# Weight ring of a float32r encoder: the four slots' start addresses moved off multiples of 256 bytes

## The chip, the cores and the metric

One Trainium2 chip, one core. The metric is the device time of one execution in microseconds (us), lower is better. The kernel before took 2029.19 us (median of three runs, 2028.7 to 2029.87).

## The reference

A two-layer encoder on 512 tokens of width 1,024. Each layer is a half-step SwiGLU feed-forward, a token mixer, and another half-step feed-forward. Each sublayer is normalised before and after, and added to the residual:

```
h = rmsnorm(x, g0);  gate, up = split(h @ w_in);  y = (silu(gate) * up) @ w_out
x = x + 0.5 * rmsnorm(y, g1)                      # four of these, w_in 1024 x 5632, w_out 2816 x 1024
x = x + rmsnorm(mla(rmsnorm(x, g2)), g3)          # layer 0: latent attention, 8 heads
x = x + rmsnorm(hgrn2(rmsnorm(x, g2)), g3)        # layer 1: gated linear recurrence, w_in 1024 x 5120
```

All in float32. Nearly all of the arithmetic is activations times weights.

## The kernel before, in words

**Products.** A float32 product is made of three float32r products: each operand is kept as a high part rounded to float32r and a low part holding the rest, and `mm3` (L634, its matmuls at L637, L638 and L639) adds w_hi·x_hi, w_hi·x_lo and w_lo·x_hi into one PSUM bank. The weight block, 128x128, is the stationary operand and the activation, 128x512 (transposed, tokens along the free dimension), is the moving one. Where the order is written out by hand, at the entry of a sublayer, the same three products are at L793, L794, L799 (all sublayers but the first) and L819, L822, L825 (the first one). The attention uses one tile of weights as the moving operand (L644 to L646).

**Weights.** They come in tiles of 128 partitions x 1,024 float32 (eight blocks of 128 columns, 512 bytes each; one tile in three of the down projection has six blocks). The SP queue loads a tile into `raw` (L482; at L507 in quarters for the first four tiles of the kernel), ScalarE rounds it into `w_hi` (L1459, quarters at L1466), and GpSimd subtracts the two and writes `w_lo` over `raw` (L563, quarters at L576). In the recurrence and at each sublayer's entry VectorE does this last step (L1978). TensorE then uses the tile for 24 matmuls and frees it (`w_free`) with the first matmul of the next tile, and SP loads the tile due three places later into the freed slot.

**Slots.** A slot holds `raw` (shared with `w_lo`) and, 4,096 bytes on, `w_hi`, 8,192 bytes in all. The ring has four slots side by side (L318 to L323). Two extra slots lie at the end of the arena and take tiles 4 and 5 of each sublayer, three more take three late tiles of the recurrence, and two hold weights made on the chip for the attention (L324 to L327). `tile_slots` (L133) assigns the tiles; all that don't go to an arena slot go round the ring.

**Addresses.** The constants come first. A pad (`below_line`, L235) brings the next buffer, the residual `xt`, to a multiple of 2,048 bytes, and since every large buffer after it has a size that is a multiple of 2,048, the operands `xg_hi`, `xg_lo`, `hid_hi`, `hid_lo` and all slots begin on one too (asserted at L265 for the arena and the ring). Weight blocks therefore begin on multiples of 512. Small buffers (`cols` and those after it) follow the ring.

**Order of the work.** Up projection: 44 tiles of 24 matmuls, eight for each k of one bank. Down projection: eight groups of 66 matmuls over three tiles. Both run in loops of four tiles or four groups. The last down group of the kernel (`final_group`, L921) runs over the two halves of the tokens, with 128x256 moving operands. Where TensorE would wait, `keep_clock` (L737) multiplies float32 constants, 128x256.

```
first = pe.matmul(ps, w_hi[slot][:, at:at + n], hi, start=start, stop=False)     # L637
pe.matmul(ps, w_hi[slot][:, at:at + n], lo, start=False, stop=False)             # L638
pe.matmul(ps, w_lo[slot][:, at:at + n], hi, start=False, stop=stop)              # L639
pool.tensor_tensor(w_lo[slot][:, 0:n], raw[slot][:, 0:n],
                   w_hi[slot][:, 0:n].bitcast(F32), ALU.subtract).then_inc(w_ready, 1)
```

Of the kernel before, what the change touches and what calls it, by code (L numbers as in the profile page):

```python
# [29 lines left out]
F32 = mybir.dt.float32  # L30
F32R = mybir.dt.float32r
# [6 lines left out]
P = 128  # L38
# [11 lines left out]
TILE = 8 * P  # L50
# [39 lines left out]
def unit_order():  # L90

    order = [("turn", 0, 0), ("turn", 0, 1)]
    for n in range(QUARTERS):
# [5 lines left out]
        if n + 1 < QUARTERS:  # L99
# [13 lines left out]
SUMMED_BY_POOL = (0, 2, 4, 6)  # L113
RING = 4
LINE = 2048
ENTRY = 4
PAIRS_OF_CHUNKS = KB // 2
PIECES = ENTRY * PAIRS_OF_CHUNKS
EXTRA = 2
# [7 lines left out]
             ("ffn", 2, 6, 7), ("hgrn", 0, 8, 9), ("ffn", 3, 10, 11)]  # L127
PAIRS_FIRST = (ENTRY + EXTRA) // 2
SIDE_ROOT, SIDE_WIDE = 6, 14
UP_LOOPS = (UP_TILES - ENTRY - EXTRA) // RING  # L130


def tile_slots():  # L133

    slots, ring = [], 0
    for kind, _, _, _ in SUBLAYERS:
        for t in range(TILES_OF[kind]):
            if ENTRY <= t < ENTRY + EXTRA:
                slots.append(RING + t - ENTRY)
            elif kind == "hgrn" and t in LATE:  # L140
# [82 lines left out]
def build(nc, x, w_up, w_down, w_mla, w_turned, w_hgrn, columns, consts, positions, out):  # L223
    ctx = ExitStack()
    with ctx:
        def sb(name, shape, dt=F32):
            return ctx.enter_context(nc.sbuf_tensor(name, shape, dt))

        def sem(name):
            return ctx.enter_context(nc.semaphore(name))  # L230
# [3 lines left out]
        ones = const[:, C_ONES:C_ONES + P]  # L234
        sb("below_line", [P, -(nc.sbuf_base + -nc.sbuf_base % 32) % LINE // 4])  # L235
        assert nc.sbuf_base % LINE == 0
        xt = sb("xt", [P, KB, SEQ])
# [20 lines left out]
        def slab(name, size):  # L258
            sb(name, [P, size // 4])
            return nc.sbuf_base - size  # L260

        arena_bytes = 2 * FB * SEQ * 4
        arena_at = slab("arena", arena_bytes)
        ring_at = slab("ring", RING * 2 * TILE * 4)
        assert arena_at % LINE == 0 and ring_at % LINE == 0  # L265
        cols = sb("cols", [P, N_COLS])
        half_cols = sb("half_cols", [P, QN_COL])
# [47 lines left out]
        o_sq = middle  # L315


        def tile_slot(n, at):  # L318
            return (nc.alloc_sbuf_tensor_at(f"raw{n}", [P, TILE], F32, offset=at),
                    nc.alloc_sbuf_tensor_at(f"w_lo{n}", [P, TILE], F32R, offset=at),  # L320
                    nc.alloc_sbuf_tensor_at(f"w_hi{n}", [P, TILE], F32R, offset=at + 4 * TILE))

        slots = [tile_slot(n, ring_at + n * 8 * TILE) for n in range(RING)]  # L323
        slots += [tile_slot(RING + n, arena_at + arena_bytes - (EXTRA - n) * 8 * TILE) for n in range(EXTRA)]  # L324
        slots += [tile_slot(RING + EXTRA + n, arena_at + n * 8 * TILE) for n in range(len(LATE))]
        MADE = len(slots)
        slots += [tile_slot(MADE + n, made_at + n * 8 * TILE) for n in range(MADE_TILES)]  # L327
        raw, w_lo, w_hi = zip(*slots)
# [23 lines left out]
        raw_full = [sem(f"raw_full{n}") for n in range(RING + EXTRA + len(LATE))]  # L352
        piece_in = [[sem(f"piece_in{q}_{g}") for g in range(ENTRY)] for q in range(PAIRS_OF_CHUNKS)]
        hi_made = sem("hi_made")
# [2202 lines left out]
```

## Time and profile before

| | |
|---|---|
| median of three runs | 2029.19 us (2028.7 to 2029.87) |
| the profiled execution's own time | 2032.39 us |
| its span, first to last instruction | 2030.6 us |
| granted TensorE clock, mean | 0.997 |
| PE busy (matmuls) | 2020.4 us, 11,182 matmuls |
| PEld busy (weight loads) | 1676.7 us |
| VectorE, ScalarE, GpSimd busy | 925.3, 714.4, 676.0 us |
| DMA | 179.49 MB, mean 88 GB/s, 27.4% of 16 engines' time on SP's queue |

A matmul's row in the profile lasts until its result has drained, and the next one starts well before that. So what a matmul costs in a stream is the distance from one start to the next, and the mean duration of a row is longer than that. PEld is the loading of stationary weights, which overlaps the matmul before.

### The profile page before, as it was taken

Reading aid. Unit: us, or ns where it says so; the run is one execution under the profiler, and the core shown is the slowest. Engines: PE = TensorE matmul, PEld = TensorE weight load, DVE = VectorE, ACT = ScalarE, POOL = GpSimd, SP = SyncE. Lnnn points to the kernel's source line nnn. Section 1 sums busy time; section 2 is a strip of 40 time slices with the busy share of each in tenths; the row PEclk is TensorE's granted clock in tenths of the full one; section 3 lists DMA queues with packets and bytes.
Section 4 is the critical chain, followed back from the end, with each engine's and each line's share of the span. In section 5 each row is a group of like instructions: output and inputs, shape, how many; then the busy total and the mean of one; then the engine's idle time right before and its main releaser. Section 6 shows DMA issues by size and latency. Waiting matters only on the chain.

```text
span 2030.6 us, 28406 instructions
## 1 busy us (share of the span) xinstructions
PE 2020.4 (100%) x11182; PEld 1676.7 (83%) x11182; DVE 925.3 (46%) x1228; ACT 714.4 (35%) x971; POOL 676.0 (33%) x310
## 2 busy tenths in 40 slices
PE   9999999999999999999999999999999999999999
PEld 7888888888888888888888888888888878888887
DVE  6433421588474343115534311476766766433212
ACT  5222232455342222224222222465655543222221
POOL 4444444220224444442544444200000024444444
PEclk9999999999999999999999999999999999999999
DMA  4233234200223223333232333222221122322332
GB/s 166 93 98 98 91 96 133 95 22 1 63 83 98 99 93 94 99 96 104 78 99 93 96 94 103 81 86 81 68 69 64 64 73 94 99 98 93 96 96 88
DMA packets 54516, 179.49 MB, mean 88 GB/s; under 512 B 6048, under 2 KB 10400, under 8 KB 54432
## 3 DMA queue, kind: packets, MB, share of 16 engines
q1 hardware_dynamic: 54000, 176.73, 27.4%
q10 hardware_dynamic: 432, 1.57, 0.2%
q8 instruction: 61, 1.00, 0.2%
q14 instruction: 23, 0.19, 0.0%
HBM read 176.18 MB, written 2.10 MB: 88 GB/s over the span
## 4 chain that ended last, share of the span: by engine, by line
PE 95%; DVE 2%; ACT 1%; issue 1%; DMA 0%; SPq 0%; DVEq 0%; ACTq 0%
PE psum L637 28%; PE psum L638 28%; PE psum L639 28%; PE psum L793 2%; PE psum L794 1%; PE psum L799 1%; PE psum L1055 1%; PE psum L1162 1%; ACT prob L1666 0%; PE psum L825 0%; PE psum L822 0%; PE psum L1242 0%; PE psum L1199 0%; PE psum L1220 0%; PE psum L1241 0%
## 5 line engine op out<-in xcount | busy, mean ns | idle before, releaser
L563 POOL TENSOR_TENSOR w_lo<-raw,w_hi 128x1024 fp32r<-128x1024 f32 (+1 forms) x276 | 648.9, 2353 | 1302.6 <-ACT w_hi L1459 1302.6
L637 PE MATMUL psum<-xg_hi,w_hi 128*128 128x512 f32 x1735 | 683.4, 394 | 1.0 <-DVE xg_lo L2300 0.5
L639 PE MATMUL psum<-xg_hi,w_lo 128*128 128x512 f32 x1735 | 676.5, 390 | 0.0
L638 PE MATMUL psum<-xg_lo,w_hi 128*128 128x512 f32 x1735 | 676.3, 390 | 0.0
L1459 ACT ACTIVATE w_hi<-raw 128x1024 fp32r<-128x1024 f32 (+1 forms) x332 | 343.1, 1037 | 839.8 <-DMA raw<-w_up 464.1
L637 PEld LDWEIGHTS psum<-xg_hi,w_hi 128*128 128x128 f32 x1735 | 326.2, 188 | 71.2 <-issue 1.6
L639 PEld LDWEIGHTS psum<-xg_hi,w_lo 128*128 128x128 f32 x1735 | 326.2, 188 | 68.5
L638 PEld LDWEIGHTS psum<-xg_lo,w_hi 128*128 128x128 f32 x1735 | 326.3, 188 | 67.1 <-issue 1.2
L637 PE MATMUL psum<-hid_hi,w_hi 128*128 128x512 f32 (+1 forms) x726 | 278.0, 383 | 0.0
L638 PE MATMUL psum<-hid_lo,w_hi 128*128 128x512 f32 (+1 forms) x726 | 277.7, 383 | 0.0
L639 PE MATMUL psum<-hid_hi,w_lo 128*128 128x512 f32 (+1 forms) x726 | 277.7, 383 | 0.0
L2024 DVE TENSOR_TENSOR t_b<-psum,r_pre 128x512 f32<-128x512 f32 x100 | 69.1, 691 | 344.5 <-PE psum L639 343.6
L2061 DVE COPY y<-psum 128x512 f32<-128x512 f32 x47 | 32.5, 692 | 389.8 <-PE psum L639 345.5
L639 PEld LDWEIGHTS psum<-hid_hi,w_lo 128*128 128x128 f32 x726 | 136.4, 188 | 26.8
L637 PEld LDWEIGHTS psum<-hid_hi,w_hi 128*128 128x128 f32 x726 | 136.4, 188 | 26.6
L638 PEld LDWEIGHTS psum<-hid_lo,w_hi 128*128 128x128 f32 x726 | 136.4, 188 | 26.4
L2031 DVE TENSOR_TENSOR t_d<-t_c,t_b 128x512 f32<-128x512 f32 x88 | 130.0, 1477 | 10.0
L2024 DVE TENSOR_TENSOR t_a<-psum,r_pre 128x512 f32<-128x512 f32 x100 | 69.1, 691 | 113.3 <-PE psum L639 111.4
L1549 ACT ACTIVATE t_c<-t_a 128x512 f32<-128x512 f32 x88 | 55.6, 632 | 133.8 <-DVE t_a L2024 133.8
L1978 DVE TENSOR_TENSOR w_lo<-raw,w_hi 128x1024 fp32r<-128x1024 f32 x56 | 69.5, 1242 | 15.9 <-ACT w_hi L1459 14.8
L2035 DVE TENSOR_TENSOR hid_lo<-t_d,hid_hi 128x512 f32 (+1 forms) x88 | 69.3, 787 | 9.4
L2072 DVE TENSOR_TENSOR sqsum<-sqsum,sq 128x512 f32<-128x512 f32 x36 | 42.3, 1175 | 32.4 <-ACT sq L1483 32.4
(258 smaller groups left out, 1617.0 us busy)
## 6 DMA issues: line engine op xcount, KB each, us to landing
raw<-w_up SPq DMA_DIRECT2D x172, 512.0 KB, 3.5
raw<-w_down SPq DMA_DIRECT2D x64, 512.0 KB, 3.5
raw<-w_hgrn SPq DMA_DIRECT2D x48, 512.0 KB, 3.5
raw<-w_down SPq DMA_DIRECT2D x32, 384.0 KB, 3.1
raw<-w_mla SPq DMA_DIRECT2D x16, 512.0 KB, 3.5
raw<-w_up SPq DMA_DIRECT2D x16, 128.0 KB, 4.6
xt<-x_t SPq DMA_DIRECT2D x8, 256.0 KB, 4.8
out<-xt SPq DMA_DIRECT2D x16, 128.0 KB, 1.7
```

The costliest lines, as they stand in the source:

```text
L563: pool.tensor_tensor(w_lo[slot][:, 0:n], raw[slot][:, 0:n], w_hi[slot][:, 0:n].bitcast(F32), ALU.subtract).then_inc(w_ready, 1)
L637: first = pe.matmul(ps, w_hi[slot][:, at:at + n], hi, start=start, stop=False)
L638: pe.matmul(ps, w_hi[slot][:, at:at + n], lo, start=False, stop=False)
L639: return first, pe.matmul(ps, w_lo[slot][:, at:at + n], hi, start=False, stop=stop)
L793: first = pe.matmul(banks[g], w_hi[tiles[g]][:, at], xg_hi[:, k, :], start=k == 0, stop=False)
L1459: act.activation(w_hi[slot][:, 0:n], raw[slot][:, 0:n], ACT.Copy).then_inc(hi_made, 1)
L1549: act.activation(t_c[:, :], t_a[:, :], ACT.Silu).then_inc(silu_done, 1)
L1978: dve.tensor_tensor(w_lo[slot][:, :], raw[slot][:, :], w_hi[slot][:, :].bitcast(F32), ALU.subtract).then_inc(lo_made, 1)
L2024: dve.tensor_tensor(dst, bank(), r_pre[:, :], ALU.mult).then_inc(drained, 1)
L2031: dve.tensor_tensor(t_d[:, :], t_c[:, :], t_b[:, :], ALU.mult).then_inc(dve_step, 1)
L2035: dve.tensor_tensor(hid_lo[:, f, :], t_d[:, :], hid_hi[:, f, :].bitcast(F32), ALU.subtract).then_inc(hidden_ready, 1)
L2072: dve.tensor_tensor(sqsum[:, :], sqsum[:, :], src, ALU.add).then_inc(sq_added, 1)
```

## The change

The four slots of the ring keep their distance of 8,192 bytes, but within them the tile begins later: slots 0 and 1 begin 16 bytes, slots 2 and 3 begin 240 bytes past the former address, and so past a multiple of 2,048. `raw`, `w_lo` and `w_hi` of a slot move together. The ring's buffer grows by 256 bytes per partition, so `cols` and the small buffers after it move up by 256. The slots in the arena get no `past` and stay, as do all activations. No instruction is added, removed or reordered.

```
+STAGGER = (16, 16, 240, 240)
+ROOM = 64
...
-        ring_at = slab("ring", RING * 2 * TILE * 4)
+        ring_at = slab("ring", RING * 2 * TILE * 4 + 4 * ROOM)
...
-        def tile_slot(n, at):
-            return (nc.alloc_sbuf_tensor_at(f"raw{n}", [P, TILE], F32, offset=at),
-                    nc.alloc_sbuf_tensor_at(f"w_lo{n}", [P, TILE], F32R, offset=at),
-                    nc.alloc_sbuf_tensor_at(f"w_hi{n}", [P, TILE], F32R, offset=at + 4 * TILE))
-
-        slots = [tile_slot(n, ring_at + n * 8 * TILE) for n in range(RING)]
+        def tile_slot(n, at, past=0):
+            room, begin = (ROOM, past // 4) if past else (0, 0)
+            whole = (nc.alloc_sbuf_tensor_at(f"raw{n}", [P, TILE + room], F32, offset=at),
+                     nc.alloc_sbuf_tensor_at(f"w_lo{n}", [P, TILE + room], F32R, offset=at),
+                     nc.alloc_sbuf_tensor_at(f"w_hi{n}", [P, TILE + room], F32R, offset=at + 4 * TILE))
+            return [tensor[:, begin:begin + TILE] for tensor in whole]
+
+        slots = [tile_slot(n, ring_at + n * 8 * TILE, STAGGER[n]) for n in range(RING)]
```

## Rows read from the trace of the kernel before

**Rows 1.** The page: busy time by engine, and the chain that ended last.

```profile
PE 2020.4 (100%) x11182; PEld 1676.7 (83%) x11182; DVE 925.3 (46%) x1228; ACT 714.4 (35%) x971; POOL 676.0 (33%) x310
...
PE 95%; DVE 2%; ACT 1%; issue 1%; DMA 0%; SPq 0%; DVEq 0%; ACTq 0%
```

**Rows 2.** Groups by line and shape, PE, whole span: count | busy us, mean ns.

```profile
L637 PE MATMUL psum<-xg_hi,w_hi 128*128 128x512 f32 x1735 | 683.4, 394 | 1.0 <-DVE xg_lo L2300 0.5 <-DVE w_lo L1978 0.3
...
L637 PE MATMUL psum<-hid_hi,w_hi 128*128 128x512 f32 x682 | 265.3, 389 | 0.0
...
L793 PE MATMUL psum<-xg_hi,w_hi 128*128 128x512 f32 x121 | 48.9, 405 | 0.6 <-ACT xg_hi L1522 0.5
...
L637 PE MATMUL psum<-hid_hi,w_hi 128*128 128x256 f32 x44 | 12.7, 288 | 0.0
```

**Rows 3.** Timeline, 300 to 306 us: start, duration; one 512-column stream with its weight loads.

```profile
300.01 0.39 PE L637 MATMUL psum<-hid_hi,w_hi 128*128 128x512 f32 x1
300.01 0.19 PEld L638 LDWEIGHTS psum<-hid_lo,w_hi 128*128 128x128 f32 x1
...
303.16 2.39 POOL L563 TENSOR_TENSOR w_lo<-raw,w_hi 128x1024 fp32r<-128x1024 f32 x1 [2.95 <-ACT w_hi L1459]
...
305.45 0.39 PE L637 MATMUL psum<-hid_hi,w_hi 128*128 128x512 f32 x1
```

**Rows 4.** Timeline, 2008 to 2009.2 us: the same operands, 256 columns moving.

```profile
2007.89 0.28 PE L637 MATMUL psum<-hid_hi,w_hi 128*128 128x256 f32 x1
2007.90 0.19 PEld L638 LDWEIGHTS psum<-hid_lo,w_hi 128*128 128x128 f32 x1
...
2008.97 0.28 PE L637 MATMUL psum<-hid_hi,w_hi 128*128 128x256 f32 x1
```

**Rows 5.** PE timeline, 397 to 405 us: a stream after a pause, and slowed.

```profile
396.74 0.40 PE L638 MATMUL psum<-xg_lo,w_hi 128*128 128x512 f32 x1
396.98 0.40 PE L639 MATMUL psum<-xg_hi,w_lo 128*128 128x512 f32 x1
...
397.67 0.62 PE L639 MATMUL psum<-xg_hi,w_lo 128*128 128x512 f32 x1
...
400.65 0.63 PE L639 MATMUL psum<-xg_hi,w_lo 128*128 128x512 f32 x1
...
403.64 0.63 PE L637 MATMUL psum<-xg_hi,w_hi 128*128 128x512 f32 x1
```

**Rows 6.** Windows: the slowed stretch; busy by engine, granted clock, DMA share, GB/s.

```profile
397.70:404.50 6.80, 6.80 (x22) 5.64 (x21) 1.16 (x6) 2.25 (x4) 3.38 (x2) 0.50 0.07 13
```

**Rows 7.** Timeline, 566 to 568.4 us: float32 keep_clock matmuls, merged.

```profile
566.30 2.32 PE L740 MATMUL psum<-const 128*128 128x256 f32 x10
```

**Rows 8.** PEld timeline, 386.5 to 388.6 us: two weight loads with no matmul between.

```profile
386.61 0.19 PEld L793 LDWEIGHTS psum<-xg_hi,w_hi 128*128 128x128 f32 x1 [0.37 <-ACT xg_hi L1522]
386.72 0.19 PEld L794 LDWEIGHTS psum<-xg_hi,w_lo 128*128 128x128 f32 x1
```

**Rows 9.** DMA issues: count, KB each, median us to landing.

```profile
raw<-w_up SPq DMA_DIRECT2D x172, 512.0 KB, 3.5
...
raw<-w_up SPq DMA_DIRECT2D x16, 128.0 KB, 4.6
```

**Rows 10.** Timeline without PE, 1800 to 1812 us: one tile's refill.

```profile
1801.88 0.33 SPq L482 DMA_DIRECT2D raw<-w_up  x1
...
1805.41 1.06 ACT L1459 ACTIVATE w_hi<-raw 128x1024 fp32r<-128x1024 f32 x1 [4.51 <-DMA raw<-w_up]
...
1806.55 2.40 POOL L563 TENSOR_TENSOR w_lo<-raw,w_hi 128x1024 fp32r<-128x1024 f32 x1 [3.17 <-ACT w_hi L1459]
```

**Rows 11.** Chain of 0 to 20 us, its longest piece: start, us, what.

```profile
3.10 4.57 DMA raw<-w_up
```

**Rows 12.** VectorE's splits (L1978): min/median/max ns, and who waited for them.

```profile
L1978 DVE TENSOR_TENSOR w_lo<-raw,w_hi x56: 1216/1224/2278, 22.6 to 1681.4; 128x1024 fp32r<-128x1024 f32 x56
...
  PE psum L637: 0.3, 1
```

## The prediction

> **What bounds the kernel.** I read the page's busy times and chain first: PE is busy for 2020.4 of 2030.6 us and holds 95% of the chain that ended last; VectorE, ScalarE and GpSimd stay under half of the span [rows 1]. So only what changes the distance between TensorE's starts, or opens a gap in them, can change the time. The groups by line and shape give the numbers of matmuls [rows 2], and the timelines the distances. In a steady stream of 512-column matmuls, 24 distances cover 300.01 to 305.45, so one is 5.44/24 = 0.2267 us [rows 3]. The reader should see in that group that the next weight load starts with each matmul and lasts 0.19, and that the distance doesn't move while GpSimd rewrites another slot from 303.16 on.
>
> Then I asked what the 226.7 ns are made of. With 256 columns nine distances cover 2007.89 to 2008.97, or 120.0 ns [rows 4]. The 256 further columns thus cost 106.7 ns, which is 2.4 columns per ns, one per cycle of the upper clock level. What is left is the same for both, 226.7 - 213.3 = 13.3 ns, or 32 cycles. In the stretch with a granted clock of 0.50, that is 1.2 GHz, seven distances cover 400.65 to 403.64, 427 ns each, which is 512 cycles and nothing besides [rows 5, 6]. And float32 matmuls of 256 columns at the upper level start every (2.32 - 0.38)/9 = 215.6 ns, if the last of the ten lasts the 0.38 that is their usual length (an estimate from the neighbouring distances), so two cycles per column and 2.2 ns over [rows 7]. So there is an extra of 13.3 ns at full rate, which is gone where the operand is read at half the rate. It could be a toll of reading, and to that an address could matter. That is the only large thing that this change can touch.
>
> **The change part by part.** Nothing is added, removed or reordered on any queue. What moves are addresses.
>
> TensorE's weight loads read the ring at 16 or 240 past 256. How many matmuls that concerns: the four groups shown, tripled because each product has three, are 3 x (1735 + 682 + 121 + 44) = 7,746 [rows 2]; the small groups of the same kind, not shown, hold 80 triples, 240; the arena slots take away two tiles of 24 in each of six sublayers (288), three late tiles (72) and 48 on weights made on the chip. That leaves about 7,580. The trace of before shows no weights at such an address, so the cost is bounded. Two loads with no matmul between start 0.11 us apart [rows 8], and loads keep up with a distance of 0.12 [rows 4]; in the 512-column stream a load has 0.227. It could become about 105 ns longer before a matmul waited. Hence my value is 0 for loading itself, and the matmul's own stream reads only activations, which stay. The two ends, kept for the range: each nanosecond on the distance is 7.58 us. The lowest that the rows know is the float32 extra, 2.2 ns in place of 13.3: -11.1 x 7,580 = -84 us [rows 3, 7]. The highest is the distance of streams that have just restarted, four in 396.74 to 397.67 or 232.5 ns: +5.8 x 7,580 = +44 us [rows 5]. I take 0 because it is what the steady rows say of every block and operand, at eight different multiples of 512.
>
> The loads of tiles write rows of 4,096 bytes that begin off 256. Landing takes 3.5 us [rows 9]. A slot's refill is issued at 1801.88, rounded from 1805.41, and ready at 1808.95 [rows 10]; the slot is due three tiles of 24 x 0.2267 after it was freed, at about 1818. So 9 us of cover hide any slower landing, and the same cover hides ScalarE's 1.06 and GpSimd's 2.40, whose operands move too; without that cover each extra microsecond per tile would be one per tile for PE. What this cover doesn't reach is the kernel's start, where a piece of 4.57 us in the chain is weights in flight [rows 11]. Bounds: 0, and the difference between the two landing times, 4.6 - 3.5 = 1.1 us [rows 9]. I take 0.3, near the lower end, because the rows become no shorter and no more numerous.
>
> There the skill has a rule against the change. The Trainium skill, "DMA: Bandwidth & Descriptors", section "How a descriptor splits into AXI transactions", says that a transaction must begin at a multiple of 256 bytes, so that a descriptor that begins off one costs an additional, partly used one. By that a piece of 1,024 bytes takes five for four, and an estimate from the page for the start is a quarter of 4.57, +1.1 us in place of 0.3. No run so far shows it.
>
> VectorE's 56 splits read and write moved slots. Their median is 1,224 and their minimum 1,216 ns, and PE waits for them once, for 0.3 us [rows 12]. Bounds 0 and 56 x 8 ns = 0.4 us; I take 0. The small buffers after the ring move by a whole 256 bytes; I take 0 for them, covered by the idle half of the engines that read them [rows 1].
>
> Sum: 0 + 0.3 + 0 = +0.3 us. The profiled execution took 2032.39 for a span of 2030.6, 3.2 above the median of 2029.19, so it comes to 2032.7 in its own terms and to 2029.5 in the median's. A half-clock stretch such as the 6.8 us one [rows 6] costs half its length; if a shift of timing makes one or avoids one, that is 3.4 us either way. The likeliest case's own range is 2026 to 2034.
>
> **Rival A: the reads collide, and the shift parts them (faster).** Weights and activations all begin on the same multiples today. If the 13.3 ns are the moving stream giving way to weight reads that hit the same part of the memory, one step of 16 bytes either way could end that. For it: the extra has no dependence on the columns, exactly the 128 columns of weights are common to both [rows 3, 4], and it vanishes where the stream leaves room [rows 5, 7]. Against it: no block or operand differs from another; and a fixed delay when weights are swapped would look the same. Price: up to 84 us, 1945 us; with half of it, 1987. By the Trainium skill, "TensorE: Matmul & The Clock Gate", section "Back-to-back issue gap", the distance would be N/2.4 + 2.5 ns, 215.8 for 512 columns. The row has 226.7, so page and trace differ, and the measurement decides; would the change restore the page's figure, an estimate from it is -82 us.
>
> **Rival B: the shift makes weight reads collide (slower).** Place: the same 7,580 matmuls. A 512-byte block that begins 16 or 240 past 256 reaches over one more boundary of 256, and the alignment of today may be the good case. For it: the distance isn't rigid; after a pause it is 0.24 and then 0.2325 on the mean of four before it settles at 0.227 [rows 3, 5], so phases between reads do matter, and most phases are worse than the settled one. Against it: the 105 ns of room. It decides from 0.5 ns per matmul, 4 us. Price up to +44 us, 2073; with half of it, 2051.
>
> **Rival C: only the start pays.** With both upper bounds, 1.1 + 0.4, it is 2030.7 (2029.2 + 1.5), which is still no difference.
>
> **How the numbers follow.** Hidden loading (and C with it): 0.47. Rival A: 0.31. Rival B: 0.22. A measurement here can tell about 0.2%, 4 us, from no change. The time is that of the likeliest case, 2029.5. The range takes in that case, rival A whole, and the milder half of B: 1945 to 2050, which leaves out about 0.12 of B and a little of A. Faster 0.31, within 0.2% 0.46, slower 0.23 (B, and an additional half-clock stretch).
>
> **What would show it.** Hidden loading: distances of 0.2267 and 0.120 in the same places, weight loads of 0.19, the 512-column rows at a mean of 389 ns. Rival A: a distance nearer 0.215 on tiles of the ring and 0.2267 still on tiles in the arena; means under 389. Rival B: means of 392 to 398, again on the ring alone. If slots at 16 and slots at 240 differ, the distance changes every two tiles. The forecast is wrong if the steady distance moves by more than half a nanosecond. It would also be wrong, at the same distance, if ScalarE's or GpSimd's rows grew by more than 9 us per tile, or if the start grew by over 4 us.

## The result and the profile after

The changed kernel takes 2032.1 us (median of 17 runs, 2031.11 to 2035.35) where the kernel before takes 2028.91 in as many (2027.4 to 2031.81). The ratio is 1.0017, 95% interval 1.001 to 1.0025: a small loss of about 3 us. The interval leaves out 1, and the loss is smaller than the 0.2% that the forecast counted as no difference. The forecast was 2029.5 within 1945 to 2050, with 0.46 on no difference.

The page of the changed kernel, first the busy times, then the groups by line and shape (count | busy us, mean ns). Four lines were added above them, so L641 is the former L637 and L797 the former L793.

```profile
PE 2019.6 (100%) x11182; PEld 1673.2 (82%) x11182; DVE 933.1 (46%) x1228; ACT 714.9 (35%) x971; POOL 677.5 (33%) x310
```

```profile
L641 PE MATMUL psum<-xg_hi,w_hi 128*128 128x512 f32 x1735 | 683.2, 394 | 1.0 <-DVE xg_lo L2304 0.5 <-DVE w_lo L1982 0.3
...
L641 PE MATMUL psum<-hid_hi,w_hi 128*128 128x512 f32 x682 | 265.3, 389 | 0.0
...
L797 PE MATMUL psum<-xg_hi,w_hi 128*128 128x512 f32 x121 | 49.4, 408 | 0.8 <-ACT xg_hi L1526 0.7
```

Against [rows 2] nothing moves but the last group, from 405 to 408 ns. That is the first trace of the loss: L797 is the entry of a sublayer, right behind a pause, and the long streams are as before. The timeline of a down projection agrees. Below are two starts of one stream, some 5.7 us apart:

```profile
299.86 0.39 PE L641 MATMUL psum<-hid_hi,w_hi 128*128 128x512 f32 x1
...
305.53 0.39 PE L642 MATMUL psum<-hid_lo,w_hi 128*128 128x512 f32 x1
```

They are 25 distances apart, and 5.67 us over 25 are 226.8 ns each, as in [rows 3]. So I looked behind the pauses. In the recurrence, small matmuls come between the tiles, and each tile of 24 begins anew. Here is the same tile (the fifth after the two in the arena, in slot 0) in both kernels, PE's timeline, starts and durations. Before:

```profile
1361.94 0.50 PE L637 MATMUL psum<-xg_hi,w_hi 128*128 128x512 f32 x1
...
1362.28 0.40 PE L638 MATMUL psum<-xg_lo,w_hi 128*128 128x512 f32 x1
...
1365.29 0.39 PE L639 MATMUL psum<-xg_hi,w_lo 128*128 128x512 f32 x1
...
1367.33 0.39 PE L639 MATMUL psum<-xg_hi,w_lo 128*128 128x512 f32 x1
```

After:

```profile
1358.58 0.50 PE L641 MATMUL psum<-xg_hi,w_hi 128*128 128x512 f32 x1
...
1358.91 0.39 PE L642 MATMUL psum<-xg_lo,w_hi 128*128 128x512 f32 x1
...
1361.94 0.39 PE L643 MATMUL psum<-xg_hi,w_lo 128*128 128x512 f32 x1
...
1364.05 0.40 PE L643 MATMUL psum<-xg_hi,w_lo 128*128 128x512 f32 x1
```

Before, 13 distances behind the pause take 3.01 us, 231.5 ns each, and the last nine 2.04 us, 226.7 ns: the stream settles. After, the first 13 take 3.03 us, 233.1 ns, and the last nine still take 2.11 us, some 234 ns (233.6 from the starts in whole ns). It settles too, but on another distance.

From the starts of all matmuls I worked out how much this is. The sum takes every float32r matmul of 512 columns that follows without a pause, so whose distance to the next start is 215 to 242 ns, and adds what it has over 226.67 ns, in the one profiled execution of each kernel. I call it the **unsettled time**:

| stretch, us | before: matmuls over 228 ns, unsettled us | after |
|---|---|---|
| 50 to 340 (feed-forward) | 0, 0.0 | 0, 0.0 |
| 340 to 600 (entry, attention) | 151, 0.9 | 371, 2.0 |
| 600 to 930 (feed-forward) | 1, 0.0 | 1, 0.0 |
| 930 to 990 (entry) | 28, 0.2 | 85, 0.5 |
| 990 to 1290 (feed-forward) | 0, 0.0 | 0, 0.0 |
| 1290 to 1700 (entries, recurrence) | 258, 1.5 | 696, 3.9 |
| 1700 to the end (feed-forward) | 0, 0.0 | 0, 0.0 |
| whole kernel, with the start | 448, 2.7 | 1161, 6.4 |

It grows by 3.8 us, where the medians differ by 3.2. The profiled spans, 2030.6 before and 2029.3 after, run the other way. The granted clock says why. The profiled execution of before ran two stretches at half clock (the windows view, granted clock third from the end), the one of [rows 6] and one at 1298.8:

```profile
1298.80:1302.20 3.40, 3.40 (x10) 2.68 (x9) 3.11 (x5) 1.79 (x3) 1.02 (x1) 0.50 0.74 294
```

The profiled execution of the changed kernel had none before its very end. Here is the place of [rows 6] in it:

```profile
397.00:404.00 7.00, 7.00 (x41) 5.97 (x40) 2.19 (x8) 2.71 (x5) 4.58 (x2) 1.00 0.24 75
```

Half of 6.8 + 3.4 us is 5.1 us, an estimate of what the two stretches cost, and 2030.6 - 5.1 + 3.8 is the 2029.3 of the span after. Half-clock stretches come and go from one execution to the next (the 17 executions of the changed kernel have mean clocks of 0.997 to 1.000 and spans of 2029.3 to 2033.5). The medians are the thing to compare.

By slot the pattern is plain. Of the tiles 9 to 39 of the recurrence, the last nine distances of each have a mean of 226.7 ns before in all 31. After, 14 of the 16 tiles in slots 0 and 1, those 16 bytes past, stay at 233.1 to 233.6 ns, and two are at 226.7. Of the 15 in slots 2 and 3, 240 past, eight are at 228.0 to 228.4 and seven at 226.7. A level is the mean of a repeating pattern of single distances. At 226.7 they are 226 or 227 ns throughout. In the changed kernel's tile above, at 233.6, they run 232, 233, 235, 234, 233, 233 and again.

### The profile page after: what moved, and what is told of

It reads as the page before. It is cut to its first block, busy times and chain, and to the rows that moved or that the text cites. A ratio compares the mean times of both kernels' runs of the same rounds, so it can differ in the third digit from the quotient of the medians.

```text
span 2029.3 us, 28406 instructions
## 1 busy us (share of the span) xinstructions
PE 2019.6 (100%) x11182; PEld 1673.2 (82%) x11182; DVE 933.1 (46%) x1228; ACT 714.9 (35%) x971; POOL 677.5 (33%) x310
## 4 chain that ended last, share of the span: by engine, by line
PE 96%; DVE 2%; ACT 1%; issue 1%; DVEq 0%; ACTq 0%
PE psum L641 28%; PE psum L642 28%; PE psum L643 28%; PE psum L797 2%; PE psum L798 1%; PE psum L803 1%; PE psum L1059 1%; PE psum L1166 1%; ACT prob L1670 0%; PE psum L823 0%; PE psum L829 0%; PE psum L826 0%; PE psum L1246 0%; PE psum L1224 0%; PE psum L1203 0%
## 5 line engine op out<-in xcount | busy, mean ns | idle before, releaser
L641 PE MATMUL psum<-xg_hi,w_hi 128*128 128x512 f32 x1735 | 683.2, 394 | 1.0 <-DVE xg_lo L2304 0.5
L641 PEld LDWEIGHTS psum<-xg_hi,w_hi 128*128 128x128 f32 x1735 | 325.9, 188 | 71.3 <-issue 1.6
L641 PE MATMUL psum<-hid_hi,w_hi 128*128 128x512 f32 (+1 forms) x726 | 277.9, 383 | 0.0
L641 PEld LDWEIGHTS psum<-hid_hi,w_hi 128*128 128x128 f32 x726 | 136.3, 188 | 26.7
L2035 DVE TENSOR_TENSOR t_d<-t_c,t_b 128x512 f32<-128x512 f32 x88 | 136.8, 1555 | 10.0
```

Source lines behind the costliest of these rows:

```text
L2035: dve.tensor_tensor(t_d[:, :], t_c[:, :], t_b[:, :], ALU.mult).then_inc(dve_step, 1)
```

## The experiments

**Theories.** *Phase:* behind a pause, a stream of matmuls falls into one of several repeating patterns of distances, and which patterns exist depends on where the weights begin. *Transfer:* tiles off 256 land or are split late, and that opens pauses. *Moved buffers:* the 256 bytes by which the small buffers move cost the time. Later, within the phase theory, two more questions: whether it is the weights' own place or the difference between their address and the activations', and whether the period is 256.

**Offsets back to 0, room kept.** `STAGGER = (0, 0, 0, 0)`.

> The change with all four offsets set to 0: slots back on multiples of 2,048, only the 256 bytes of room stay, so the small buffers after the ring keep their new place. Phase theory (after a pause a stream of matmuls falls into one of several repeating patterns, and which ones exist depends on where the weights begin): as before, ratio 1.000 (0.9995 to 1.0005), and after each pause the distance is back at 226.7 ns within about ten matmuls. Moved-buffers theory (the small buffers' new place costs the time): 1.0017, as the change.

Measured: 0.9999 (0.999 to 1.0008), 226.7 ns in all 31 tiles, unsettled time 2.6 us. The moved buffers cost nothing that can be told from no change, so that theory is out.

**All four slots at 16, all four at 240.** `STAGGER = (16, 16, 16, 16)` and `(240, 240, 240, 240)`.

> All four slots begin 16 bytes past. Phase theory: in the recurrence and the attention all ring tiles that follow a pause stay at 233.2 ns, not only those of slots 0 and 1; some 20 more tiles of 24 matmuls at +5 ns are 2 to 3 us on top of the change's 3.2, so the ratio is 1.0025 to 1.003. The feed-forward streams stay at 226.7. Transfer theory (loads, rounding and splitting of tiles that begin off 256 are late, and open pauses): the same 1.0017 as the change, since 16 and 240 are alike off 256, and the additional time is in gaps of over 240 ns.

> All four slots begin 240 bytes past. Phase theory: after a pause the tiles are at 228.4 or back at 226.7 ns, none at 233.2; unsettled matmuls cost 1 to 1.5 us more than before, ratio 1.0003 to 1.001. Transfer theory: 1.0017, as the change.

Measured: 1.0028 (1.0017 to 1.0039) and 1.0003 (0.9993 to 1.0013). The unsettled times are 7.9 and 3.2 us. With 16 the tiles behind pauses are at 233.1 to 233.6 or at 226.7 (13 of 31 at the latter, more than I had expected); with 240 at 228.0 to 228.4 or 226.7, none near 233. The transfer theory has both equal and falls: the two intervals don't meet. The change is a mixture of the two.

**The extra slots at 16 too.** With all of the ring at 16:

```
-slots += [tile_slot(RING + n, arena_at + arena_bytes - (EXTRA - n) * 8 * TILE) for n in range(EXTRA)]
+slots += [tile_slot(RING + n, arena_at + arena_bytes - (EXTRA - n) * 8 * TILE, 16) for n in range(EXTRA)]
```

> All four ring slots and also the two extra slots at the end of the arena begin 16 bytes past. In the kernels so far each feed-forward sublayer passes, after the pause at its entry, over two tiles in those aligned extra slots, settles there at 226.7 ns, and the ring's tiles go on in that pattern. Phase theory: without aligned tiles behind the pause the stream goes into the ring in the slow pattern and keeps it, 233.2 ns, for up to 1,488 matmuls in each of four feed-forwards: +6.5 ns each is up to +39 us, ratio up to 1.02; at the least one of the four locks, +10 us. If a stream returns to 226.7 by itself, as e2. Transfer theory: 1.0017 to 1.002.

Measured: 1.0198 (1.018 to 1.0217), 2069.27 us. Moving two slots in the arena costs 32 us more than the ring alone at 16. The windows of 200 us within the four feed-forwards show it in their count of matmuls (the stretch and its length, then busy us and count by engine, PE first):

```profile
100.00:300.00 200.00, 200.00 (x859) 161.96 (x858) 73.25 (x99) 50.20 (x57) 85.14 (x36) 1.00 0.30 94
700.00:900.00 200.00, 200.00 (x859) 161.97 (x858) 54.36 (x67) 48.80 (x54) 86.14 (x37) 1.00 0.31 92
1050.00:1250.00 200.00, 200.00 (x884) 165.59 (x883) 63.15 (x75) 50.48 (x56) 86.82 (x38) 1.00 0.32 97
1760.00:1960.00 200.00, 200.00 (x859) 161.96 (x858) 65.99 (x82) 48.19 (x53) 85.46 (x36) 1.00 0.30 93
```

A window holds 884 matmuls at 226.7 ns, counting those that reach over its ends, and 859 at 233.3. Three of the four feed-forwards fell into the slow pattern and kept it to their end; the third caught the fast one in this execution and kept that. So both patterns are stable with 16, and what follows the pause decides. The weight loads take 161.96 / 858 = 0.189 us each in a slow window and 165.59 / 883 = 0.188 in the fast one. In the kernel with the change the two aligned tiles behind each entry settle the stream at 226.7 before it reaches the ring, which is why its feed-forwards lose nothing.

**Ring and extra slots at 240.** The same edit with 240.

> Ring and extra slots all begin 240 bytes past. Phase theory: a feed-forward that leaves its entry's pause in the 228.4 ns pattern keeps it: +1.7 ns for 1,488 matmuls, 2.5 us each, so 0 to +10 us in the four, ratio 1.000 to 1.005 and most likely 1.003 to 1.005; 226.7 only where it settled by chance. Were 16 and 240 alike in themselves, it would be 1.02 as with 16.

Measured: 1.0022 (1.0012 to 1.0032), and the single runs range from 2029.3 to 2037.06, wider than before's 2027.47 to 2033.6. That is in the range that was expected, below its likeliest part (1.003 to 1.005). In the profiled one three feed-forwards are at 226.7 and the last is at 228.3:

```profile
1760.00:1960.00 200.00, 200.00 (x877) 164.32 (x876) 59.37 (x73) 50.91 (x57) 87.71 (x38) 1.00 0.31 94
```

**Two scans, four offsets in one kernel each.** `STAGGER = (32, 64, 96, 128)` and `(48, 160, 192, 224)`.

> The four ring slots begin 32, 64, 96 and 128 bytes past; extra slots aligned. Read is the settled distance of each slot's tiles behind pauses in the recurrence. Phase theory in its period-256 form (only the place within 256 bytes counts): the levels differ by slot, at least one of them sticks above 226.7 ns, and the further from 0 the less alike the aligned case; the feed-forwards stay at 226.7 since they enter the ring settled. Boundary theory (a 512-byte block that touches a third multiple of 256 costs more, wherever it begins): all four slots stick at the same level, 228 to 233 ns.

> The four ring slots begin 48, 160, 192 and 224 bytes past. Phase theory: again levels by slot, near 240 (224) like the 240 slots, 228.4 or 226.7 ns; 48 is between 16 and 64. Boundary theory: one level for all. If a slot shows a level under 226.7 ns, the aligned start is not the best one, and a version with all slots there would beat both kernels.

Measured: 2077.26 and 2071.7 us, one execution each, beside 2029.85. The levels differ by slot, so the boundary theory falls. But the feed-forwards do not stay at 226.7, against what was expected of both: 858 and 863 matmuls in the 200 us from 100 on. Both enter the ring settled, and lose the fast pattern within the first tile there. The window of the first scan:

```profile
100.00:300.00 200.00, 200.00 (x858) 161.05 (x858) 71.38 (x98) 50.81 (x57) 84.96 (x36) 1.00 0.30 92
```

**Everything 32 bytes up, slots 16 past that.** This kernel and the next tell the weights' own place from its difference to the activations'.

```
-sb("below_line", [P, -(nc.sbuf_base + -nc.sbuf_base % 32) % LINE // 4])
+sb("below_line", [P, -(nc.sbuf_base + -nc.sbuf_base % 32) % LINE // 4 + 8])
```

> All operand buffers and slots are moved 32 bytes up, and ring and extra slots begin 16 past that: weights at 48 past a multiple of 2,048, activations at 32. If the distance between weight and activation addresses decides, it is the kernel with ring and extra slots at 16 again: feed-forwards locked at 233.2 ns, span near 2063. If the weights' own place within 256 decides, it shows what slot 0 of the second scan (48 past) shows, in the feed-forwards too.

Measured: 2073.6 us, one execution, beside 2029.85; its span, 2071.8, is above the expected 2063, which was that of an execution with one fast feed-forward. Weights are at 48 and activations at 32. All four feed-forwards are locked at 859 matmuls in 200 us (233.3 ns), and of the 31 tiles nine are at 226.7 and the rest at 233.1 to 233.6: the two levels of a difference of 16. Slot 0 of the second scan, at 48 beside activations at 0, is at 233.3 or 233.4 in all of its eight tiles, never at 226.7. That speaks for the difference, but the feed-forwards alone would fit both.

**Everything 32 bytes up, slots too.** As the kernel above, with all offsets 0.

> All operand buffers and all slots are moved up by the same 32 bytes. Distance theory (only weight address minus activation address counts, within 256): as the kernel before, 884 matmuls per 200 us in every feed-forward, 226.7 ns after every pause, span 2027 to 2032. Own-place theory (the weights' own place counts): as slot 0 of the first scan, 233.3 ns everywhere, span near 2075.

Measured: 2027.68 us, one execution, beside 2030.66 for the kernel before. All 31 tiles are at 226.7, and every feed-forward has its 884:

```profile
100.00:300.00 200.00, 200.00 (x884) 165.68 (x883) 75.13 (x99) 52.87 (x60) 88.78 (x38) 1.00 0.31 97
```

Slot 0 of the first scan has weights at the same 32, with activations at 0, and is at 233.1 to 233.6. So it is the difference between the two addresses that counts; that is shown for 0, 16 and 32 bytes, and not tried at the others.

**Period and grain.** `STAGGER = (4, 8, 256, 272)` with `ROOM = 128`, and `(12, 20, 208, 248)`.

> The four ring slots begin 4, 8, 256 and 272 bytes past, with 512 bytes of room. Phase theory with a period of 256: behind pauses slot 2 (256) settles at 226.7 ns every time as at 0, slot 3 (272) is like 16, 233.2 or 226.7. With a longer period (512 or 2,048) slot 2 would stick at another level, such as the 233.3 of 128. Slots 0 and 1 tell the grain: if pieces of 16 bytes count, 4 and 8 are partly like 0 and partly like 16; a level under 226.7 would be a gain.

> The four ring slots begin 12, 20, 208 and 248 bytes past. Phase theory: 12 and 20 are near 16 and stick at 233 or settle at 226.7; 248 is between 240 (228.4 or 226.7) and 0; 208 is between 192 (228.9) and 224 (233.3). No theory says a level under 226.7; one would be a better kernel.

Measured: 2050.05 and 2068.01 us, one execution each, beside 2027.29. Behind pauses slot 2 at 256 is at 226.7 in all its seven tiles and slot 3 at 272 at 233.1 to 233.3 or 226.7, so the period is 256 or a part of it, and the table excludes a smaller one. Four bytes are enough to lose: 232.3 ns. That 12 and 20 behave like 16 held in part only. 20 is at 233.3 in every tile. 12 has a level of its own besides, about 230 with single distances of 224 and 236 by turns, but it does hold the fast pattern: one of its eight tiles behind pauses is at 226.7, and so is the first ring tile of the first feed-forward, which is entered settled and begins and ends here, 24 distances in 5.44 us:

```profile
40.47 0.39 PE L641 MATMUL psum<-xg_hi,w_hi 128*128 128x512 f32 x1
...
45.91 0.39 PE L641 MATMUL psum<-xg_hi,w_hi 128*128 128x512 f32 x1
```

The next tile, at 20, is at 233 and ends it. 248 isn't between 240 and 0 either.

All offsets together: the mean over all distances of a slot's tiles in an up projection (the spread is between the four feed-forwards), and, behind pauses, the mean of a tile's last nine distances. Beyond 0, 16 and 240 each comes from one execution of one kernel.

| weights past activations, bytes | in the feed-forwards, ns | behind pauses, ns |
|---|---|---|
| 0, 256 | 226.7 | 226.7 in every tile |
| 16, 272 | 226.7 or 233.3 (272: 227.0) | 226.7, or 233.1 to 233.6 |
| 240 | 226.7 or 228.3 | 226.7, or 228.0 to 228.4 |
| 4, 8, 12 | 232.3, 230.7, 229.5 to 229.8 | 232.0 to 232.4, 230.2 to 230.9, 226.7 to 233.4 |
| 20, 32, 48, 64 | 233.2 to 233.5 | 233.1 to 233.7 |
| 96, 128 | 233.7 to 234.0, 232.1 to 233.3 | 233.9 to 234.3, 232.1 to 233.9 |
| 160, 192 | 233.4, 228.9 | 233.3, 228.9 |
| 208, 224, 248 | 231.7, 233.3, 233.3 | 231.8 to 233.3, 233.3 to 233.6, 233.3 |

And the kernels with several executions, unsettled time (of one execution) against ratio:

| kernel | unsettled us over before | ratio less 1, times 2030 us |
|---|---|---|
| offsets 0 | -0.1 | -0.2 |
| all 240 | +0.5 | +0.6 |
| the change | +3.8 | +3.5 |
| ring and extra 240 | +2.6 | +4.5 |
| all 16 | +5.2 | +5.7 |
| ring and extra 16 | +35.8 | +40 |

The quantity that was found behind the pauses goes with the size of all six. The two kernels with moved extra slots depend on which patterns an execution catches, and in one place the order fails: ring and extra at 240 have less unsettled time than the change and the greater ratio. Taken by themselves, their profiled executions fit: 2064.97 and 2032.23 us are 34.8 and 2.4 above the medians of before (2030.17 and 2029.85), with 35.8 and 2.6 unsettled. Of the kernels with one execution, the scans at 32 to 128 and at 48 to 224 have 46 and 40 us more unsettled time than before and took 47 and 42 us more, the kernel with weights at 48 and activations at 32 has 45 and took 44.

No version beats the kernel before: 0 and 256 have the shortest distance and the only one that doesn't depend on the pause. The kernel with everything 32 bytes up can't be told from it by one execution.

## Why the prediction was right, and where not

The likeliest case was no difference, and the measured ratio of 1.0017 is just within it (its interval reaches 1.0025); the time is inside the range. But the reason given for it, that loading stays hidden wherever the weights lie, is refuted, and that the number held is luck: for ring and extra slots at 16 the same reasoning would have said no difference too, and the ratio was 1.0198. Point by point:

- **The bound, and the steady distance.** Right. 226.7 ns in every long stream, no instruction moved, and the result hangs on the distance between starts alone.
- **"My value is 0 for loading itself"**, because a load has 0.227 us and needs 0.12. This is the step that failed. It treated the weight load as a thing that either fits or not. The runs show that the distance between starts grows though the load stays well inside its room (0.189 us at a distance of 0.2333), by up to 7.4 ns at 96 bytes. The loss is zero where the addresses agree within 256, and at 12, 16, 240 and 272 also where the stream was settled before. The term is +3.5 us (0.0017 x 2029), in place of 0.
- **"What the steady rows say of every block and operand, at eight different multiples of 512."** Those rows said nothing on the question: eight multiples of 512 are one and the same place within 256. I should have asked which places the trace covers before taking agreement as evidence.
- **The end at +44 us.** Its row was the right one. 232.5 ns behind a pause [rows 5] is an unsettled stream, and 233 ns is what most offsets settle on. The kernel with the extra slots at 16 comes to +40 us, and the scan at 32 to 128, with +47, goes past that end.
- **Rival B** had the mechanism, phases between reads and a settled distance, but a wrong place: "the same 7,580 matmuls". Only some 700 more than before are unsettled, those between a pause and the next one. That so little of it came true was decided by two arena slots that the change left alone, which neither this rival nor the likeliest case took into account. A sign that the prediction named, a distance that differs between slots at 16 and at 240, did appear, behind pauses only. Its reason, a block reaching over one more boundary of 256, is refuted by the scans, since 16, 96 and 192 reach over it alike and give three levels.
- **Rival A** is wrong in sign. Agreement of the addresses is the best case, not the collision. The 13.3 ns remain unexplained: no offset gave a shorter mean. The Trainium skill's figure in "TensorE: Matmul & The Clock Gate", section "Back-to-back issue gap", 215.8 ns for 512 columns, which the section gives for matmuls without weight loads between them, was not reached at any of the 18 other offsets. The Trainium skill, on the same page in "Step-by-step: what each phase is for", says that loading the next weights doesn't take read bandwidth from the running matmul, thanks to two independent read ports. For float32r the runs show that the two reads are not indifferent to each other: the kernels with weights at 48 and at 32, activations at 32 in both, differ in these 16 bytes of the slots alone and by 46 us. Whether it is read bandwidth that one takes from the other is not shown.
- **The start, +0.3 us**, and +1.1 by the Trainium skill's rule on descriptors off 256 ("DMA: Bandwidth & Descriptors", section "How a descriptor splits into AXI transactions"). Neither can be told. For tiles landing stays at 3.5 us (3.6 for the recurrence's, from 3.5). The piece of [rows 11] is no longer in the chain of the start. For the first pieces landing is shorter than in [rows 9], as the line below shows, but it is 4.4 to 4.6 in the two kernels with aligned slots and 4.0 to 5.2 in the eleven others, more scatter than either term. The hundredth matmul of the first feed-forward starts at 29.0 us, before at 29.8.

```profile
raw<-w_up SPq DMA_DIRECT2D x16, 128.0 KB, 4.2
```

- **VectorE's splits, 0.** Right, by the line's own view of the changed kernel, against [rows 12]:

```profile
L1982 DVE TENSOR_TENSOR w_lo<-raw,w_hi x56: 1217/1224/2276, 22.4 to 1680.1; 128x1024 fp32r<-128x1024 f32 x56
```

- **A half-clock stretch more or less.** It occurred as allowed for, and two stretches are the reason that one profiled execution alone would have called the change faster by 1.3 us.

## What to carry to other kernels

Put stationary and moving operands of float32r matmuls at the same place within 256 bytes; here a few bytes between them cost up to 3% of the matmuls that follow a pause, and with most differences of every matmul. Where they can't agree, try 16 or 240 and two tiles that do agree right behind each pause; in the scans at 32 to 224 bytes the aligned tiles didn't keep the feed-forwards fast. When a profile is to bear out that addresses don't matter, list first which places within 256 bytes it really holds.

## What was not expected of the hardware

A stream of matmuls has more than one stable distance for the same instructions and addresses: 226.7 and 233.3 ns with weights 16 bytes past, 226.7 and 228.3 with 240. With all slots at one of these offsets it keeps the one that it caught, for over 1,400 matmuls, and hands it on from slot to slot, until a pause deals anew. Weights that begin 4 bytes past cost 5.6 ns over 226.7 in every matmul. And what matters isn't where either operand is, but how far apart they are within 256: both moved by 32 bytes is the kernel before. Why of all offsets off 256 only 12, 16, 240 and 272 were seen to allow the fast pattern, and what the 13.3 ns over one column per cycle are, stays open. The runs don't separate the load of the same product from that of the next one, and a stream without weight loads wasn't tried.
